# Products that nothing reads, run by TensorE in seven of its waits

## Time and profile before

| | us |
|---|---|
| three executions | 1206.04, 1208.00, 1209.63 (median 1208.0) |
| the profiled execution, its own time | 1209.83 |
| its span, from first to last instruction | 1207.9 |
| mean granted TensorE clock | 0.941 |
| busy: PE, DVE, ACT, POOL | 1097.2, 887.1, 645.2, 121.7 |

### The profile page before, as it was taken

One profiled execution on the slowest core, in us unless ns is written; L12 is line 12 of the kernel. 1 busy time (PEld: TensorE's weight loads), 2 busy tenths in 40 slices (PEclk: granted clock), 3 DMA queues, 4 the chain that ended last, 5 costly groups with the idle time before them and its releaser, 6 DMA issues.

```text
span 1207.9 us, 15260 instructions
## 1 busy us (share of the span) xinstructions
PE 1097.2 (91%) x5316; PEld 831.7 (69%) x5316; DVE 887.1 (73%) x1125; ACT 645.2 (53%) x799; POOL 121.7 (10%) x158
## 2 busy tenths in 40 slices
PE   5999999789899999999983899999999999999980
PEld 4776776567777777777762888778877777777750
DVE  5253555867788999999994462553688999999975
ACT  5133434421347888888871321232267888888841
POOL 2000000021211000000004100000111000000005
PEclk9998999889979999999996899999879999999995
DMA  8632222220259999999974633233169999999935
GB/s 302 189 125 70 79 79 70 70 88 13 75 190 356 378 408 396 397 397 411 410 283 158 255 106 104 70 105 105 71 224 359 402 391 396 410 397 396 418 123 208
DMA packets 77598, 286.35 MB, mean 237 GB/s; under 512 B 16647, under 2 KB 16647, under 8 KB 61164
## 3 DMA queue, kind: packets, MB, share of 16 engines
q1 hardware_dynamic: 65212, 241.64, 52.6%
q0 software_dynamic: 8608, 30.95, 7.9%
q10 hardware_dynamic: 3728, 13.11, 2.8%
HBM read 266.79 MB, written 20.20 MB: 238 GB/s over the span
## 4 chain that ended last, share of the span: by engine, by line
PE 83%; DVE 9%; ACT 2%; DMA 2%; issue 2%; POOL 1%; ACTq 0%; POOLq 0%; SPq 0%; DVEq 0%; PEldq 0%
PE ps L1558 25%; PE ps L1560 25%; PE ps L1559 24%; PE ps L1887 2%; DVE w_split L911 2%; PE ps L1540 1%; ACT w_split L605 1%; PE ps L1803 1%; DVE arena L1277 1%; DMA arena<-y_rows_dram,arena 1%; PE ps L1645 1%; DVE arena L932 1%; DVE x_sb L1329 1%; PE ps L1911 1%; DVE arena L1105 1%
## 5 line engine op out<-in xcount | busy, mean ns | idle before, releaser
L911 DVE TENSOR_TENSOR w_split<-ring,w_split 128x1024 fp32r<-128x1024 f32 x452 | 540.9, 1220 | 87.5 <-ACT w_split L605 75.4
L605 ACT CAST w_split<-ring 128x1024 fp32r<-128x1024 f32 x452 | 472.2, 1051 | 195.1 <-PE ps L1560 191.5
L1558 PE MATMUL ps<-w_split,hT 128*96 128x512 f32 (+1 forms) x960 | 391.4, 408 | 14.2 <-DVE hT L1377 6.2
L1560 PE MATMUL ps<-w_split,hT 128*96 128x512 f32 (+1 forms) x960 | 383.8, 400 | 0.0
L1559 PE MATMUL ps<-w_split,hT 128*96 128x512 f32 (+1 forms) x960 | 383.6, 400 | 0.0
L1558 PEld LDWEIGHTS ps<-w_split,hT 128*96 128x96 f32 (+1 forms) x960 | 165.0, 172 | 79.3 <-issue 11.6
L1560 PEld LDWEIGHTS ps<-w_split,hT 128*96 128x96 f32 (+1 forms) x960 | 164.1, 171 | 63.4
L1559 PEld LDWEIGHTS ps<-w_split,hT 128*96 128x96 f32 (+1 forms) x960 | 165.4, 172 | 57.5 <-issue 0.3
L1558 PE MATMUL ps<-hT,w_split 128*128 128x512 f32 (+1 forms) x384 | 147.5, 384 | 5.7 <-issue 4.1
L1559 PE MATMUL ps<-hT,w_split 128*128 128x512 f32 (+1 forms) x384 | 145.0, 378 | 0.0
L1560 PE MATMUL ps<-hT,w_split 128*128 128x512 f32 (+1 forms) x384 | 144.8, 377 | 0.0
(11 more groups left out here) (218 smaller groups left out, 846.4 us busy)
## 6 DMA issues: line engine op xcount, KB each, us to landing
ring<-in_exp_w_gate SPq DMA_DIRECT2D x64, 1024.0 KB, 10.5
ring<-in_exp_w_up SPq DMA_DIRECT2D x64, 1024.0 KB, 10.7
ring<-in_exp_w_down SPq DMA_DIRECT2D x64, 1024.0 KB, 11.7
ring<-in_w_in_even SPq DMA_DIRECT2D x14, 1024.0 KB, 10.1
y_rows_dram<-arena ACTq DMA_DIRECT2D x32, 384.0 KB, 6.9
ring<-in_w_in_odd SPq DMA_DIRECT2D x12, 1024.0 KB, 7.3
ring<-in_w_out_even SPq DMA_DIRECT2D x4, 1024.0 KB, 4.8
h_rows_dram<-arena POOLq DMA_DIRECT2D x8, 512.0 KB, 4.5
```

The source lines that it names most:

```text
L605: s.copy(hi_of(c), raw(c)).then_inc(hi_ready, 1)
L911: v.tensor_tensor(lo_of(c), raw(c), hi_of(c).bitcast(F32), ALU.subtract).then_inc(lo_ready, 1)
L1558: mm(out, a[0], b[0], start=start, stop=False)
L1560: return mm(out, a[0], b[1], start=False, stop=stop)
```

## The change

A helper `keep_busy(n, bank)` is added to TensorE's stream. It issues n matmuls of fp16 with 512 columns each, `ones16` by a broadcast column of `later`, into a PSUM bank that is free at that moment. No semaphore is raised and nothing reads the result; each starts a fresh sum. It is called with 20 ahead of the first turn and 8 behind the third, 8 behind the turned gate rows, 4 and 3 around the ranks of the last tile in each layer's routing, 14 ahead of the last down product of each layer, and 56 ahead of and 14 behind the first turns of the odd mixer: 148 products in all. Nothing is removed and no other engine's stream is changed.

```diff
--- before.py
+++ after.py
@@ -1549,9 +1549,16 @@
                 pe.wait_ge(tr_act, tiles_copied(n, TT - 1, True))
                 pe.wait_ge(tr_dve, tiles_copied(n, TT - 1, False))
 
+            def keep_busy(n, bank):
+
+                for _ in range(n):
+                    mm(ps[:, bank, :], ones16[:, :], later[:, 0:1].broadcast_to([P, 512]), start=True, stop=True)
+
             pe.wait_ge(consts_ready, 7)
+            keep_busy(20, 7)
             for t in range(TT - 1):
                 turn_h(0, t)
+            keep_busy(8, 7)
 
             def mm3(out, a, b, start, stop):
 
@@ -1631,6 +1638,7 @@
                     last = nc.tensor.transpose(ps[:, 1, c:c + HEADS], gate_rows[0:HEADS, row, j * P:(j + 1) * P],
                                                ident[0:HEADS, 0:HEADS])
             last.then_inc(gate_cols_full, 1)
+            keep_busy(8, 3)
             pe.wait_ge(gate_cols_ready, 1)
             pe.wait_ge(job_act, EARLY // 2)
             pe.wait_ge(job_dve, EARLY // 2)
@@ -1863,7 +1871,9 @@
                 ranks(2)
                 logits(3)
                 gather_first(2)
+                keep_busy(4, 0)
                 ranks(3)
+                keep_busy(3, 0)
                 for r in range(TT):
                     last = mm(ps[:, 7, RANK0:RANK0 + E], ones16[:, :], member[:, r, :],
                               start=(r == 0), stop=(r == TT - 1))
@@ -1953,6 +1963,7 @@
                 n = n0 + E - 1
                 step(n, 1, step_chunk(l, E - 1), None, None, last=True)
                 turn_act(n)
+                keep_busy(14, 0)
                 down(n, 1, step_chunk(l, E), None)
 
                 o = over[l]
@@ -2016,8 +2027,10 @@
                     pe.wait_ge(chunk_done, PIECE * (ODD_BASE + 1))
                     pe.sem_inc(odd_full, 1)
 
+            keep_busy(56, 0)
             turn_h(2, 0)
             turn_h(2, 1)
+            keep_busy(14, 7)
             pe.wait_ge(tr_act, tiles_copied(2, 1, True))
             pe.wait_ge(tr_dve, tiles_copied(2, 1, False))
             first_piece(0)
```

## The result

Four executions of the changed kernel took 1190.63 to 1195.31 us, median 1192.45; the kernel before beside it 1207.02 (1205.03 to 1209.63, four executions). The ratio is 0.988, 95% interval 0.9851 to 0.991. The forecast was 1198.0, range 1193 to 1205: right in sign and short in size.

A forecast was written before the change was run, and what follows sets the result against it. TensorE, busy 91% of the span and partly at low clock, was taken as the bound. Terms 1.0 + 2.3 + 2.0 + 2.9 + 0.6 + 1.5 = 10.3 us, off the median, gave 1198 us; range 1193 to 1205.

The forecast's parts named there:

- The price of a filler and where it is free: At every place: one filler costs 0.21 us at full clock, 0.43 at low clock, nothing while it lies inside a wait.
- First turns 1.0: Start of the kernel: fillers around the first turns bring job 0 to full clock, gaining 1.0 us (bounds -0.5 and 1.4).
- gates 2.3: Behind the turned gate rows: eight free fillers let dense products run at full clock, gaining 2.3 us (bounds 0 and 2.6).
- Last expert 2.9 and 0.6: Last down products: layer 0's fillers are free, gaining 2.9 us; layer 1's outlast the wait by 1.05 us, gaining 0.6.
- entrance 1.5: Entrance of the odd mixer: the 56 useless, the 14 give the first piece full clock, gaining 1.5 us.
- DVE sets the start of expert 1: Routing: DVE, not the clock, sets when expert 1 begins, so the gate product's 2.5 us are hidden.
- Routing, 1.0 a layer: Each layer's routing: the last tile's gather ends earlier, gaining 1.0 us (1.85 at best, -0.9 at worst).
- The dips that the change does not touch can fall anew.: Low-clock stretches (0.50) at places without fillers may fall differently in each execution; the sum had no term for them.
- The fillers as an obstacle (3): Rival: broadcast-column products neither hold nor raise the clock and outlast waits, costing 5.0 us in all: 1213; chance 0.06.
- nothing measurable (4): Rival: fillers hold the clock, but dips elsewhere grow or the gain is hidden behind DVE: 1207; chance 0.10.
- Half of it (1): Rival: clock falls despite fillers at gates, entrance, routing, or other engines take early gains back before 300 us: 1203; chance 0.22.
- The rule on transposes (2): Rival: transposes never count for the clock, so dips return between first turns and at the entrance: 1200; chance 0.06.

The follow-up runs named there:

- e2: Kernel before with only the fillers at the first turns (20 and 8) and behind the gate rows (8): 1203.42 us, ratio 0.9978 to the kernel before.
- e5: The whole change without the 56 fillers at the entrance of the odd mixer: 1193.12 us, ratio 0.9888 to the kernel before.
- e6: The whole change with 88 instead of 56 fillers at the entrance of the odd mixer: 1190.46 us, ratio 0.9876 to the kernel before.
- e10: The whole change with DVE's selection of the last four experts moved behind L1370: 1193.95 us, ratio 0.9909 to the kernel before.
- e3: Kernel before with only the 4 and 3 fillers in each layer's routing: 1200.02 us, ratio 0.9946 to the kernel before.
- e13: The whole change plus eight fillers ahead of the slot_index products of the last twelve experts: 1197.74 us, ratio 0.9934 to the kernel before.
- e11: The whole change plus 8, 8, 16 and 12 fillers ahead of the waits for the attention heads' turned outputs: 1192.56 us, ratio 0.9886 to the kernel before.
- e12: e11 with 88 fillers at the odd mixer's entrance and 8 instead of 14 at layer 1's last expert: 1189.26 us, ratio 0.9871 to the kernel before.
- e8: The whole change with 13 float32 128x128 transposes replacing the 8 fillers behind the gate rows: 1190.78 us, ratio 0.9881 to the kernel before.
- e9: The whole change with each 512-column filler replaced by eight products of 16 columns: 1205.92 us, ratio 1.0007 to the kernel before.
- e1: The kernel before, run and profiled once more with no edit: 1205.11 us, ratio 0.9993.

## Why the prediction was right and where it was wrong

- **The price of a filler and where it is free.** Right. The 20 took 6.7 us and ended near 10.7, the first turn was 0.9 late and job 0 did not start later; the eight at the gates left 0.7 idle. Two waits were overrun, as the prediction allowed: the last expert of layer 1, by 0.7 us (3.19 from turn to down product instead of 2.47; 1.05 forecast), and the picks in the routing. DVE's L1270 waited 0.83 us for the ranks in layer 0 and 1.04 in layer 1, against 0.29 in both before. So 0.5 and 0.75 us were lost there, out of the 1.5 allowed for.
- **First turns 1.0, gates 2.3.** 0.9 and 2.6 in the profile; e2 has 1.0 to 4.3 us for both by its interval, and shows that the gain reaches the end.
- **Last expert 2.9 and 0.6, entrance 1.5.** 2.8, 0.7 and 1.9. That the 56 would be useless was right (e5), and why, the 7.54 us still idle, too (e6).
- **DVE sets the start of expert 1.** Right: the wait for L1370 grew from 0.27 to 1.82, and e10 moved it. The gate product's 2.5 us was hidden as said. What I missed there is a small piece: with the clock back, DVE too lost pauses, 0.44 us of them a wait for ACT's L605, and the stretch from L1364 to L1370 took 13.90 or 13.91 instead of 14.24 to 14.67 in every layer with fillers in the routing, 0.8 a layer.
- **Routing, 1.0 a layer.** The term was too small: 2.0 us for both layers, and e3 measured 6.5 for the routing fillers with all that follows from them. Up to expert 1 it was 1.8 in layer 0 and 3.4 in layer 1; of the latter a part is a dip behind the logits that was 6.8 us long before and 3.4 after, and over the passes this length varies.
- **"The dips that the change does not touch can fall anew."** The step that failed most, and with it the range. The sum has no term for the dips near 376 and 912, 1.6 us each: it counts them at nothing, as luck. They were not: ten of ten times there without the routing fillers, two of fourteen with them. Both together are worth 2.7 us on average (2 x 1.6 x 12/14). What e13 shows is that timing decides. What I only argue is why it was so regular before: in the ten the small products came 20.3 to 21.4 us after the clock had come back from the dip of the routing, since the work from there on has a fixed length; the fillers brought the clock back earlier and broke that distance (29.1 us in layer 0 after the change). Where the last dip lay further back, both outcomes occur, in layer 0: a dip at a distance of 35.3 us (e5) and of 45.1 (e11), none at 43.9 (e12). Why a given distance brings a dip stays open.
- **The sum and the range.** With 0.8 x 2 and 2.7 added the sum would have been 14.6, and 1207.0 less that, 1192.4. Two steps of the working do not come out. Fourteen products at 0.2 are 2.8 and not 2.9. The upper bounds of all terms add up to 13.2, which off the median of 1208.0 gives 1194.8 and not 1193. With that bound the median would have missed the range by 2.35 us and not by 0.55: that the miss is so small is luck.
- **Rivals.** The fillers as an obstacle (3) and nothing measurable (4) fell with the ratio. Half of it (1) fell in e2 and in the profile after. The rule on transposes (2) fell in e8, for the place where it was tried. Rival 3's premise, that products of a broadcast column might not hold the clock, is true of 16 columns (e9) and false of 512.

## What to carry to other kernels

Look up, for each wait and each run of narrow products, how much dense work stands in the low-clock stretch behind it: that, not the wait, is what fillers can win, and they are free as long as they end within the wait. Where another engine sets the pace next, the clock buys nothing. Removing one low-clock stretch can spare a later one (e3) or bring one (e11), so put a price on those that look untouched, and take several profiles before adding more fillers: 44 more of them in free waits (e11) bought 5.5 us by 300 us and nothing that can be measured at the end.

## What the runs showed of the hardware

- Wide products kept the clock up, narrow ones did not: eight of 16 columns for each of 512 left the clock low as without fillers (e9), and it fell within 3.6 us of the first of 48 products of one column in both layers of all five passes without working routing fillers.
- Thirteen float32 transposes of 128x128 held the clock as well as eight products of 512 columns in fp16 (e8: 1.00 from 94 to 110 us, with either).
- A filler whose operand is one column broadcast to 512 and whose weights are ones holds the clock: 1.00 from 94.5 to 101.5 us, where it was 0.50 for 6.8 us before. At full clock eight of them took 1.91 us, and 0.38 of that is the last one's own length, so one costs about 0.22.
- The same program has its low-clock stretches at different places and of different lengths from one execution to the next: near 230 us, two of 6.8 us in the one trace of the kernel before and one of 17.1 in the other (e1). This goes with a spread of single executions of some 4 us either way (1201.75 to 1209.63 over the runs of the kernel before).
